# Order of the gather's last columns and of the slot-number spread around the first two experts' products

## What is computed

```python
gates = g_onehot[:, :, None] * (g_w[:, None] * e_gate)[:, None, :]
for gi in range(MOE_GROUPS):
    hg = jnp.einsum('td,edf->tef', t, w_gate[gi])
    hu = jnp.einsum('td,edf->tef', t, w_up[gi])
    act = jax.nn.silu(hg) * hu * gates[:, gi, :, None].astype(t.dtype)
    out = out + jnp.einsum('tef,efd->td', act, w_down[gi])
```

## Time and profile before

| | before |
|---|---|
| median of three executions | 768.54 us |
| profiled execution, its own time | 768.63 us |
| its span | 766.4 us |
| around the span | 2.2 us |
| TensorE busy | 735.6 us (96%) |
| VectorE busy | 273.5 us (36%) |
| ScalarE busy | 140.7 us (18%) |
| moved by DMA | 246.67 MB |

### The profile page before, as it was taken

One profiled execution on the slowest core, in us unless ns is written; L12 is line 12 of the kernel. 1 busy time (PEld: TensorE's weight loads), 2 busy tenths in 40 slices (PEclk: granted clock), 3 DMA queues, 4 the chain that ended last, 5 costly groups with the idle time before them and its releaser, 6 DMA issues.

```text
span 766.4 us, 8322 instructions
## 1 busy us (share of the span) xinstructions
PE 735.6 (96%) x3178; PEld 342.8 (45%) x3178; DVE 273.5 (36%) x654; ACT 140.7 (18%) x347; POOL 27.0 (4%) x49
## 2 busy tenths in 40 slices
PE   8999999999999999889999999999999999988996
PEld 5445565664333333233445554484333333323444
DVE  1213341354326323223222464263435423322323
ACT  3000231321111111110221144232111111110131
POOL 2400000000000000000000000000000000000000
PEclk9999999999999999999999999999999999999998
DMA  9997241949999999999999690238999999999911
GB/s 345 318 347 286 107 165 59 422 179 404 421 419 422 421 419 422 421 421 419 385 293 287 260 370 6 80 141 318 422 420 423 421 420 421 422 420 422 402 70 55
DMA packets 49192, 246.67 MB, mean 322 GB/s; under 512 B 4520, under 2 KB 5640, under 8 KB 24576
## 3 DMA queue, kind: packets, MB, share of 16 engines
q1 hardware_dynamic: 46928, 241.03, 79.7%
q0 software_dynamic: 2048, 5.07, 2.0%
q10 hardware_dynamic: 176, 0.02, 0.0%
HBM read 245.04 MB, written 2.63 MB: 323 GB/s over the span
## 4 chain that ended last, share of the span: by engine, by line
PE 68%; DMA 15%; SPq 9%; issue 3%; DVE 2%; ACT 1%; POOLq 0%; POOL 0%; DVEq 0%; ACTq 0%
PE bank L618 27%; PE bank L872 17%; SPq L416 9%; PE bank L889 8%; DMA weights<-in_moe_w_up_dram 7%; DMA weights<-in_moe_w_down_dram 7%; PE bank L902 2%; PE bank L849 2%; PE bank L1040 1%; PE bank L602 1%; DMA residual<-in_x_dram 1%; PE bank L881 1%; PE bank L657 1%; PE bank L677 1%; PE bank L1098 1%
## 5 line engine op out<-in xcount | busy, mean ns | idle before, releaser
L872 PE MATMUL bank<-weights,expert_rows 128*64 128x512 f32 x1024 | 227.9, 594 | 14.1 <-DMA weights<-in_moe_w_up_dram 14.1
L618 PE MATMUL bank<-weights,normalised 128*128 128x512 f32 (+1 forms) x528 | 226.1, 582 | 2.7 <-DMA weights<-in_even_w_in_dram 1.2
L618 PEld LDWEIGHTS bank<-weights,normalised 128*128 128x128 f32 x528 | 98.1, 190 | 111.7 <-issue 109.4
L872 PEld LDWEIGHTS bank<-weights,expert_rows 128*64 128x64 f32 x1024 | 75.2, 137 | 158.0 <-issue 157.3
L889 PE MATMUL bank<-weights,hidden_turned 128*64 128x512 f32 x256 | 58.8, 598 | 1.3 <-DVE hidden_turned L1753 0.6
L889 PE MATMUL bank<-weights,hidden_turned_odd 128*64 128x512 f32 x256 | 58.8, 598 | 0.5 <-DMA weights<-in_moe_w_down_dram 0.5
L1339 ACT ACTIVATE gate_tanh<-bank 128x256 f32<-128x256 f32 x32 | 12.4, 386 | 199.1 <-PE bank L872 199.1
L1783 DVE TENSOR_TENSOR gather_onehots<-bank,expert_outputs 128x512 fp32r<-128x512 f32 x32 | 22.1, 692 | 55.4 <-ACT expert_outputs L1209 55.2
L1209 ACT ACTIVATE expert_outputs<-bank 128x512 fp32r<-128x512 f32 x32 | 19.1, 597 | 123.7 <-PE bank L889 123.7
L1753 DVE COPY hidden_turned<-bank 128x256 f32<-128x256 f32 x16 | 6.8, 424 | 84.6 <-PE bank L881 84.6
L1753 DVE COPY hidden_turned_odd<-bank 128x256 f32<-128x256 f32 x16 | 6.8, 425 | 81.1 <-PE bank L881 81.1
(11 more groups left out here) (249 smaller groups left out, 598.0 us busy)
## 6 DMA issues: line engine op xcount, KB each, us to landing
weights<-in_moe_w_gate_dram SPq DMA_DIRECT2D x64, 1024.0 KB, 18.5
weights<-in_moe_w_up_dram SPq DMA_DIRECT2D x64, 1024.0 KB, 20.6
weights<-in_moe_w_down_dram SPq DMA_DIRECT2D x64, 1024.0 KB, 22.6
weights<-in_even_w_in_dram SPq DMA_DIRECT2D x5, 2048.0 KB, 29.4
weights<-in_ple_w_gate_dram SPq DMA_DIRECT2D x4, 2048.0 KB, 30.9
weights<-in_even_w_out_dram SPq DMA_DIRECT2D x2, 2048.0 KB, 19.4
weights<-in_odd_w_qkv_dram SPq DMA_DIRECT2D x2, 2048.0 KB, 20.7
weights<-in_odd_w_out_dram SPq DMA_DIRECT2D x4, 1024.0 KB, 22.2
```

Of the source, the lines that this page charges most:

```text
L618: mm = pe.matmul(B[bank][:, 0:width], XT[:, k, tok(t)], w[:, k, :], start=(k == 0), stop=(k == KD - 1))
L872: mm = pe.matmul(bank[j * BLK:(j + 1) * BLK, :].rearrange("p (m f) -> p m f", m=2), rows[:, k, :], W[:, slots, a:a + FF // 2], start=(k == ...
```

## The change

Of the four banks that `gathered(1, 1)` finishes, banks 4 and 5 are now finished before `first_rows(1)`, and banks 6 and 7 after it. `spread` is cut in two: `spread_slots` writes the slot numbers to bank 2 in place of bank 6 and runs before `other_rows(0)`; it waits until ScalarE has read banks 0 and 2. `spread_gates` writes the gate weights to bank 7 and stays between `other_rows(0)` and `other_rows(1)`, with the wait for the gates and for VectorE's copies. ScalarE reads the slot numbers from bank 2, at the same place in its list. No instruction is added or removed.

```diff
-                def gathered(group, t):
+                def gathered(group, t, ks=range(4)):
...
-                    for k in range(4 * group, 4 * group + 4):
+                    for k in [4 * group + n for n in ks]:
...
-                def spread():
+                def spread_slots():
+
+                    pe.wait_ge(sem("rows_by_act"), 4 * l + 2)
+                    for c in range(4):
+                        pe.matmul(B[2][:, tok(c)], RT[:, 404 + c:405 + c].to_broadcast([P, P]), ident, start=True, stop=True)
+
+                def spread_gates():
 
                     pe.wait_ge(sem("gates_ready"), l + 1)
-                    pe.wait_ge(sem("rows_by_act"), 4 * (l + 1))
                     pe.wait_ge(sem("rows_by_dve"), 4 * (l + 1))
-                    for c in range(4):
-                        pe.matmul(B[6][:, tok(c)], RT[:, 404 + c:405 + c].to_broadcast([P, P]), ident, start=True, stop=True)
...
-                gathered(1, 1)
+                gathered(1, 1, (0, 1))
                 first_rows(1)
+                gathered(1, 1, (2, 3))
+                spread_slots()
                 other_rows(0)
-                spread()
+                spread_gates()
                 other_rows(1)
...
-                copy(SROW.rearrange("p c s -> p (c s)"), B[6][:, :])
+                copy(SROW.rearrange("p c s -> p (c s)"), B[2][:, :])
```

## The result

The changed kernel is slower. Over 20 executions its median is 773.53 us, against 770.79 us over 20 of the kernel before, and the ratio of their times is 1.0040 with a 95% interval of 1.0023 to 1.0056, or 3.1 us. One of the 20 of before took 1528.15 us and is left out of the ratio (without it the median is 770.74). Predicted were 768.9 us, 0.3 us slower, in a range of 767.1 to 770.3.

A forecast was written before the change was run, and what follows sets the result against it. The weight stream was taken to bound each layer's end. The hole moves to the next issue and grows by 0.16 us a layer, 2 x 0.16 = 0.3 us over 768.54, giving 768.9 us, range 767.1 to 770.3.

The forecast's parts named there:

- TensorE as the bound: Rival: TensorE, not the stream, decides; the idle 0.56 us and its rounding stay in each layer, 769.7 us; chance 0.07.
- B: Weight issue of two halves freed by `first_rows(1)`; forecast at 171.06 instead of 172.20, closing its hole of 0.87 us.
- C: Weight issue of two halves freed by `other_rows(0)`; forecast at 177.34, 1.71 us late, with a new hole of 1.03.
- rival 4: TensorE's clock falls in the new gap, `other_rows(0)` 1.5 us later; 771.9 us, or 770.4 in one layer alone; chance 0.05.
- C is ready at: Issue at 177.34 plus 1.70 us gives 179.04, against the end of the data ahead at 178.01: hole of 1.03.
- D: Weight issue of two halves freed by `other_rows(1)`; forecast at about 181.9, ready at 183.6, with no hole.
- chain to the expert rows: Copies after the gather's last bank that `other_rows(0)` waits for: 1.56 us, `spread_slots` filling 1.00, TensorE idle for 0.56.
- A: Weight issue of two halves freed by `first_rows(0)`, into an empty queue, at 166.35 in layer 0; start of the stream.
- 0.16 as forecast: Net delay of the weight stream in each layer: the moved hole grows from 0.87 to 1.03 us.
- The rule set beside the rows: Skill page's first byte at some 0.6 us: no hole before or after the change, 768.6 us; chance 0.05.
- a rival only on the side of gain: The hole nearly closes, as a queue not yet empty may take up work faster; 766.8 to 768.1 us; chance 0.23.

The follow-up runs named there:

- before again: The kernel before run against itself for a second trace, nothing changed; ratio 0.9999 (0.9979 to 1.002).
- changed again: The changed kernel repeated beside the kernel before, for a second trace; ratio 1.0034 (1.0012 to 1.0055).
- the kernel with TensorE late in the loop: The kernel before with four idle products (1.0 us) per layer between expert 0's down and expert 2's gate and up products; ratio 1.0008.

## Why the prediction was wrong

**What held.** The stream of weights decides, and not TensorE. A whole microsecond of idle products in each layer's loop moved the ends by 0.7 in both layers together and the time at equal clock by 0.4, where TensorE as the bound would give 2.0. The hole moved from B to C: 1.08 and 0.81 us lost at C, 1.03 forecast. TensorE waits for the expert rows behind the last bank, 0.56 us, the forecast to a hundredth. `spread_slots` and its new wait stall nothing. The clock did not fall in the new gap, so rival 4 was wrong too, although the time came out on its side.

**The step that failed** is the rule by which an issue leaves no hole: "C is ready at" the issue plus 1.70 us, compared with the end of the data ahead. The 1.70 were measured on an empty queue, and that is right for a queue that is nearly empty. As a bound for a queue that still has data it was never tested: the kernel before has no issue between 1.1 and 2.8 us, as the second table shows, and the prediction put a step at 1.70 between the two. By it D was to lose nothing, and 0.55 and 0.74 us came (0.67 and 0.89 in the second trace), 1.3 us in all. B was to lose nothing either, and 0.29 and 0.42 stayed, but these cost nothing of their own: they move the end of B's data towards C's, and C's hole is smaller by as much. With C issued at 11.27 and B's data ending at 1.70 + 2 x 4.98 = 11.66 the rule gives 11.27 + 1.70 - 11.66 = 1.31 us, and measured at B and C together are 1.37 and 1.23. I had written that a later release "would have to be over 1.7 late to starve a queue that has two halves left". D was 1.1 late, and lost; 0.22 late was enough in layer 0 of an experiment.

**A term that was mis-sized.** Cutting the gather's run in two was priced at nothing. Eight products take 2.27 us; the two fours take 1.29 (168.39 - 167.10) and 1.19 (173.17 - 171.98), so the cut costs 0.21 (0.23 in layer 1). The chain to the expert rows took 1.61 us (174.78 - 173.17), forecast 1.56. With these C came 11.27 us after A instead of the forecast 10.99. D came 15.94 instead of 15.5, a further 0.1 later because `spread_gates` alone takes 1.09 (179.46 - 178.37) and not 0.98.

**The sum by what was measured.** In the three stretches the change loses 1.92 us in layer 0 and 1.97 in layer 1 and the kernel before 0.89 and 0.81 (from 418, 322, 426 and 428 GB/s and the like), a difference of 1.03 and 1.16. The prediction's own sum comes to the same once its two faults are put in: 0.16 as forecast, 0.28 for C's later issue, and 0.55 and 0.74 at D make 0.99 and 1.18. The ends are 1.45 and 1.87 us later than the mean over both traces of before, which leaves 0.4 and 0.7 us. These are not in the rate of the stream. From 22 to 196 us after A it is the same in both kernels, first the change, then before:

```profile
189.21:363.21 174.00, 166.63 (x800) 60.77 (x796) 61.02 (x136) 20.81 (x39) 0.00 (x0) 1.00 1.01 421
```

```profile
188.35:362.35 174.00, 166.68 (x800) 60.88 (x798) 61.56 (x137) 20.82 (x39) 0.00 (x0) 1.00 1.01 421
```

They are in how far the sixteen DMA engines end apart. In the trace each transfer of 1 MB has sixteen landings, one for each step of its semaphore, and TensorE starts 0.04 to 0.05 us after the last of them. These are the landings, after A, of the transfer that the last eight down products wait for, layer 0 and 1:

| | mean of the sixteen | last less mean |
|---|---|---|
| before | 197.76, 197.56 | 1.34, 0.98 |
| before again | 197.63, 197.71 | 1.05, 0.87 |
| changed | 198.65, 198.75 | 1.69, 1.69 |
| changed again | 199.24, 198.99 | 1.26, 1.70 |

The mean of the sixteen is 0.96 and 1.12 us later in the changed kernel's first trace than over both of before, which is what the stream lost (1.03 and 1.16). The last one lags the mean by 0.49 and 0.77 more, which is the rest. Over both traces of each kernel the means alone would give 2.5 us in the two layers together, the ends with the lag in them 3.5, and the 32 executions of the changed kernel at equal clock 3.7 to 3.8. So the lag is likely a part of the cost. But it varies by itself, too: the kernel with TensorE late in the loop, which loses no more than before, has 1.46 and 1.18. And it is not simply carried along from the issues: for the transfer that lands about 28 us after A it is 1.69 and 1.81 before, 1.13 and 2.32 in the changed kernel. How the change enlarges it is not shown.

The landings also tell what a loss at D looks like. In the steady stream each landing comes 2.48 us after that of the transfer before. In layer 0 of before, fifteen of the sixteen keep this at D's first transfer and one comes 1.5 us late. In the changed kernel fourteen could have landed by 20.96 us after A, but ten did, and the next came at 21.75. With the slow packets at D this reads as single engines that stall for about a microsecond, one of them or several. What decides whether an engine stalls while data are still queued stays open; no run here changes it alone.

**The rule set beside the rows.** The prediction weighed the Trainium skill's page "DMA: Bandwidth & Descriptors", by whose "Specifications" the first byte comes some 0.6 us after the issue, and set it aside for the dip at B. The runs say the same, and more strongly: with 2.2 to 2.8 us of data queued there is still a loss, where the rule has none. In these traces the first packet of A starts 0.95 to 0.99 us after the issue in all kernels with transfers of 1 MB, and most of the packets that start in the next half microsecond take 0.5 to 1.1 us in place of 0.31.

**The chances.** Slower by over 0.3% had 0.06, of which 0.05 was for the clock. The cost of a short queue was treated as a rival only on the side of gain (that it might take up work faster), never on the side of loss. A bound taken from one row far away should have widened the range on both.

## What to carry to other kernels

Where a stream of transfers sets the end, look at how much is queued at each issue and not only at whether the queue runs dry: here an issue of 2 x 1 MB cost nothing with 2.8 to 3.0 us of data ahead of it, if the issue before it had lost nothing, and up to 1.05 us with 2.2. Look too at the last of a transfer's sixteen landings and not only at the mean rate. Before work is moved ahead of a release, check that the releases behind it keep that margin; closing a hole of 0.9 us at one release was paid for twice at the next two. Don't buy an earlier release with smaller transfers before the smaller transfer itself has been timed.

## What was not expected of the hardware

- The stream can lose up to 1.05 us at an issue with 2.2 us of data still to move, 0.89 with 2.84 where it had lost some at the issue before, and nothing with 2.82 to 2.96 where it had not. Moving one issue by 0.22 us cost 0.61 us of stream in one layer and 0.02 in the other of one trace, and 1.8 us of time at equal clock over twelve executions.
- The DMA engines are busy in such a loss: at D the DMA share is 1.00 at 375 GB/s, and 24 of 229 packets of 8 KB take over 0.45 us in place of 0.31.
- The sixteen landings of a transfer of 1 MB end 2.0 to 2.6 us apart at the end of each mixture of the kernel before and 2.9 to 3.4 in the changed one.
- Transfers of 0.5 MB in place of 1 MB, eight halves cut in two in each layer and nothing else, cost 1.1% of the whole kernel (0.9% at equal clock).
- Cutting a run of eight gather products in two costs TensorE 0.21 us (2.27 for eight, 1.29 and 1.19 for the fours).
- The granted clock's stretches at the lower level over small products ahead of the gathers differ from one execution to the next, none to 17.1 us of them in the profiled ones here. With 0.53 us for 0.001 of mean clock they account for most of the 3 to 9 us between the fastest and the slowest execution of a kernel, and the change costs 3.8 us (within 0.4) at equal clock.
